# Chunked attention in a macaron block: probabilities laid by query block, whole-unit sums, two score units in a row, pool product in column halves

## The chip, the cores and the metric

The kernel runs as one program on all 8 cores of a Trainium2 chip. Each core works on 2,048 tokens of one of two sequences of 8,192, and on a halo of 512 tokens before them that it computes again; no core waits for another. The metric is the device time of the slowest core in microseconds (us).

## What is computed

One layer of a hybrid encoder block, D_MODEL 1024, with two feed-forward half steps around a mixer:

```
x = x + 0.5 * SwiGLU_1(RMSNorm(x))
h = RMSNorm(x);  u = h @ W_in          # pool channels (512) | q (512) | k (512) | v (512)
A = per-group trailing means (windows 2/4/8/16) - self, per-group 128x128 map (pool_w), per-channel scale
B = attention, 8 heads of 64, chunk of 64 queries over its own and the 8 previous chunks,
    scores * 64**-0.5 + clipped relative-position bias, softmax, @ v
merged = sigmoid(h W_g + b_g)[A] * (A @ W_bp) + sigmoid(h W_g + b_g)[B] * (B @ W_ba)
x = x + merged @ W_out
x = x + 0.5 * SwiGLU_2(RMSNorm(x));  out = RMSNorm(x)
```

A key block that lies before the start of the sequence counts for nothing in the softmax.

## The kernel before, in words

Activations are held transposed: channels on the 128 partitions, tokens along the free dimension, in 512-column halves `s` = 0, 1. A core does a halo tile H (512 tokens, only far enough to have keys, values and pool carry) and two tiles A and B of 1,024 tokens. Each tile goes through `ffn_up`, `ffn_down`, `w_in_phase`, `attention`, `gates_phase`, `w_out_phase`, `ffn_up`, `ffn_down`. Weights stream through a ring of five slots, loaded by POOL's queue and cast to bf16 on the way (`load_slot`). Every operation is recorded in program order by `Prog.op`, which also works out the waits: each engine then runs its own list strictly in the order in which it was recorded, and waits on semaphores for what its operation reads or overwrites. So the order in which the Python code calls things is the order on each engine.

**The attention stretch** (function `attention`, L906 on) is the place of the change. For each half `s` and each pair `p` of heads there are five units `u` (table `UNITS`), that is 40 units in a tile, taken in 8 rounds of five. A unit is 512 score columns for each of two heads `e`: one to two key blocks of 128 keys against 128 to 512 queries. Its steps:

- scores (`issue_S`, L927): for each head a matmul with 64 contraction rows, the two heads in the upper and lower half of the array's rows (form 64*128), into two of the PSUM banks 0 to 3 (`SB`, alternating by unit);
- the bias is added in place by DVE (L935) over 128 or 256 columns of each head;
- exp by ACT (L939), 1,024 columns, into one of four probability buffers (two in `Pt`, two in `ftmp`);
- for four of the five units DVE clears a 64x64 corner of each head (`issue_zero`, L947);
- products (`issue_PV`, L965): 64 output channels each for the two heads in the left and the right half of the array's columns (form 128*64). One matmul gives probabilities times values (bank 4), another gives the sums of the probabilities (bank 5), by 64 columns of ones that stand between the values of two heads in `Vt` (192 columns for a pair of heads). A key block of the halo has the flag of the halo (0 or 1) there instead of ones. After the fifth unit ACT takes Ln of the sums (L976) and Exp of its negative (L978), and one round later DVE multiplies (`divide`, L980).

In the gaps the same engine is given other work: the 16 products of the first gate (`gate` in `dense_chunks`, L878, in column halves 128*64), each cut in four chunks of four matmuls, `d(k)` issues `k` chunks. A gate accumulates in bank 6 or 7 (`DB`); its first chunk takes the bank by `nxt("dense", 2)`, which alternates; after its fourth chunk DVE copies the bank to SBUF (L884), and only then may the next user of that bank write. The eight products of the pool mixer (`pool_one`, `pool_w`, L400 form 128*128, with ACT's L849 behind) take a bank by the same alternation. `tick()` lets queued side work of DVE go.

`in_v` (L744 on) makes `Vt`: ACT copies the values (L747) and, before the change, ones or the flag (L750).

Of the kernel before, what the change touches and what calls it, by code (L numbers as in the profile page):

```python
# [26 lines left out]
VROW = 768  # L27
# [157 lines left out]
def build_nc():  # L185
# [12 lines left out]
    with es:  # L198
# [9 lines left out]
        Vt = sb("Vt", [128, KT_BLOCKS, VROW], BF16)  # L208
        biasT = sb("biasT", [128, 8, 256], F32)
# [18 lines left out]
        ones64 = cct[:, 384:448]  # L228
# [58 lines left out]
        B_cc = Buf("cc")  # L287
        B_g32 = Buf("g32")
# [446 lines left out]
        def in_v(mt, s, tb, sl):  # L735
            full = mt["full"]
            vs = (mt["blk0"] + s * 4 + tb) % KT_BLOCKS
            b = nxt("bank", NBANK)
            t0 = s * 512 + tb * 128
            mm_group(bank_ap(b),  # L740
                     [(hs[:, kc, t0:t0 + 128] if full else hh[:, kc, tb * 128:(tb + 1) * 128],
                       ring[:, sl, kc * 512:(kc + 1) * 512]) for kc in range(8)],
                     [(B_h[kc][s] if full else B_hh[kc]) for kc in range(8)] + [B_ring[sl]], b)
            vview = Vt[:, vs, :].rearrange("p (a c) -> p a c", c=192)  # L744
            vheads = Vt[:, vs, :].rearrange("p (a t d) -> p a t d", t=3, d=64)[:, :, 0:3:2, :]
            bview = bank_ap(b).rearrange("p (a e d) -> p a e d", a=4, e=2)
# [106 lines left out]
        UNITS = [([(-1, 0, 4)], (0, 128, 128), True),  # L853
# [51 lines left out]
        def attention(mt):  # L905
# [7 lines left out]
            def issue_S(i):  # L913
# [5 lines left out]
                def fn(t):  # L919
                    ins = None  # L920
                    pc = 0
                    for (dj, q0, nq) in segs:
                        col = ((base + dj) % KT_BLOCKS) * 128
# [5 lines left out]
                        pc += n  # L929
# [13 lines left out]
            def issue_zero(i):  # L943
                pi = state[i]
                if UNITS[units[i][2]][2]:
                    zap = P_aps[pi].rearrange("p (e t) -> p e t", e=2)[0:64, :, 448:512]
                    P.op("dve", lambda e: e.memset(zap, 0.0), writes=[B_P[pi]])  # L947

            def issue_PV(i):
# [4 lines left out]
                pap = P_aps[pi]  # L954

                def fn(t):
                    ins = None
                    pc = 0
                    for (dj, q0, nq) in segs:
                        vs = (base + dj) % KT_BLOCKS  # L960
                        n = nq * 128
                        for half in range(2):
                            for e in range(2):
                                l0 = p * 192 + (64 if half else 128 * e)
                                ins = t.matmul(ps[64 * e:64 * e + 64, (OB[half] * 512 + q0 * 128):(OB[half] * 512 + q0 * 128 + n)],  # L965
                                               Vt[:, vs, l0:l0 + 64], pap[:, e * 512 + pc:e * 512 + pc + n],
                                               start=(u == 0), stop=(u == 4), skip_group_check=True)
                        pc += n
                    return ins
                P.op("pe", fn, reads=[B_P[pi]] + [B_v[(base + dj) % KT_BLOCKS] for dj, _, _ in segs],  # L970
# [62 lines left out]
            issue_zero(n - 1)  # L1033
# [223 lines left out]
```

How the kernel before makes its waits and increments, by code:

```python
        def emit(engname, eng, tail=None):  # L1199
            for fn, waits, ev, is_dma in P.ops[engname]:
                for k, v in waits:
                    eng.wait_ge(sems[k], v)
                ins = fn(eng)
                ins.then_inc(sems[ev[0]], 16 if is_dma else 1)
            if tail is not None:
                tail(eng)
# [4 lines left out]
                def tail(e):  # L1211
                    for k in P.cnt:
                        if k.startswith("st"):
                            e.wait_ge(sems[k], P.cnt[k])
```

## Time and profile before

| what | value |
|---|---|
| median of 3 runs | 1517.97 us (1517.25 to 1522.94) |
| the profiled execution | 1512.99 us |
| its span on the slowest core (4) | 1511.4 us; other cores 1506.5 to 1511.1 |
| TensorE (PE) matmul busy | 1471.4 us, 97% |
| VectorE (DVE) busy | 540.9 us, 36% |
| ScalarE (ACT) busy | 462.7 us, 31% |
| chain that ended last | PE 91%, DMA 3%, DVE 3%, ACT 2% |

The busy time of PE comes from modelled ends of matmuls and includes pauses of a tenth of a microsecond; the starts of consecutive rows say more. A few matmul records are missing from a trace.

### The profile page before, as it was taken

What the parts mean: (1) busy time and instruction counts of PE and PEld (TensorE: products, weight loads), DVE (VectorE), ACT (ScalarE), POOL (GpSimd) and SP (SyncE); (2) the same over time, 40 slices, a digit from 0 to 9 for tenths busy, and PEclk for the clock granted to TensorE, in tenths of its full rate; (3) what the DMA queues carried; (4) which work ended last, traced back from release to release, by engine and by line L of the source; (5) the groups of instructions that cost most, each with busy time, mean ns of one, the idle gap of its engine ahead of it and who ended that gap; (6) DMA issues with size and microseconds to landing.
All of it is one profiled execution on the core that took longest, in us unless ns stands there. A gap on an engine that the chain in (4) does not pass through costs nothing.

```text
span 1511.4 us, 20500 instructions; the slowest of 8 cores (1506.5 to 1511.4 us)
## 1 busy us (share of the span) xinstructions
PE 1471.4 (97%) x7460; PEld 671.6 (44%) x7598; DVE 540.9 (36%) x872; ACT 462.7 (31%) x696; POOL 66.3 (4%) x129
## 2 busy tenths in 40 slices
PE   6999999999999999999999999999999999999997
PEld 2444444444444444444444444444444444444445
DVE  2323424222536554323245321223626555222124
ACT  3313112211358634213222311111357534111112
POOL 0000000000000000000000000000000000000000
PEclk9999999999999999999999999999999999999999
DMA  9853345998640454543264983344430643442323
GB/s 195 190 97 65 58 86 84 188 182 145 111 88 2 67 102 90 109 81 67 42 140 80 191 214 55 56 77 74 93 61 2 106 87 60 84 78 48 60 54 112
DMA packets 32482, 142.89 MB, mean 95 GB/s; under 512 B 2816, under 2 KB 5248, under 8 KB 21888
## 3 DMA queue, kind: packets, MB, share of 16 engines
q0 software_dynamic: 18000, 115.09, 43.3%
q1 hardware_dynamic: 14384, 26.48, 5.4%
q8 instruction: 63, 1.03, 0.3%
q14 instruction: 35, 0.29, 0.1%
HBM read 248.25 MB, written 8.39 MB: 170 GB/s over the span
## 4 chain that ended last, share of the span: by engine, by line
PE 91%; DMA 3%; DVE 3%; ACT 2%; issue 1%; another core or an unknown queue 0%; DVEq 0%; SPq 0%; ACTq 0%; POOLq 0%
PE ps L400 79%; PE ps L388 4%; PE ps L878 3%; DMA xs<-xT 2%; PE ps L965 2%; PE ps L927 1%; DMA ring<-wst 1%; DVE hs L505 1%; DVE ps L935 1%; ACT Pt L939 1%; PE ps L456 1%; ACT ftmp L939 0%; PE ps L433 0%; DVE ftmp L460 0%; DVE xs L662 0%
## 5 line engine op out<-in xcount | busy, mean ns | idle before, releaser
L400 PE MATMUL ps<-hs,ring 128*128 128x512 bf16 x3596 | 800.8, 380 | 6.1 <-DMA ring<-wst 2.2
L400 PEld LDWEIGHTS ps<-hs,ring 128*128 128x128 bf16 x3672 | 359.8, 98 | 437.6 <-issue 7.3
L400 PE MATMUL ps<-areg,ring 128*128 128x512 bf16 (+1 forms) x1953 | 426.4, 372 | 1.8
L585 DVE TENSOR_TENSOR areg<-ftmp,ps 128x512 bf16<-128x512 f32 x198 | 135.8, 687 | 524.3 <-PE ps L400 475.2
L400 PEld LDWEIGHTS ps<-areg,ring 128*128 128x128 bf16 x2004 | 195.7, 98 | 221.2 <-issue 1.0
L583 ACT ACTIVATE ftmp<-ps 128x512 f32<-128x512 f32 x198 | 118.2, 597 | 506.6 <-PE ps L400 475.1
L318 POOL DMA_DIRECT2D ring<-wst x125 | 66.1, 530 | 1386.5 <-PE ps L400 965.9
L599 DVE SCALAR_TENSOR_TENSOR xs<-ps,xs 128x512 f32<-128x512 f32 x69 | 47.6, 690 | 165.9 <-PE ps L400 134.1
L445 ACT ACTIVATE sqt<-xs 128x512 bf16<-128x512 f32 x56 | 35.2, 629 | 216.8 <-DVE xs L599 216.8
L935 DVE TENSOR_TENSOR ps<-ps,biasT 128x512 f32<-128x512 f32 (+1 forms) x80 | 46.9, 588 | 84.8 <-PE ps L927 84.8
L505 DVE SCALAR_TENSOR_TENSOR hs<-xs,cvt,rtmp 128x512 bf16<-128x512 f32 x80 | 54.6, 746 | 36.4 <-ACT rtmp L501 36.4
L878 PE MATMUL ps<-hs,ring 128*64 128x512 bf16 x512 | 67.5, 385 | 0.0
L422 ACT ACTIVATE sqt<-xs 128x512 bf16<-128x512 f32 x53 | 32.2, 626 | 73.7 <-DVE xs L1096 40.6
L939 ACT ACTIVATE Pt<-ps 128x1024 bf16<-128x1024 f32 x40 | 40.7, 1021 | 16.2 <-DVE ps L935 15.2
L388 PE MATMUL ps<-areg,ring 128*128 128x512 bf16 x202 | 45.2, 379 | 0.2
L939 ACT ACTIVATE ftmp<-ps 128x1024 bf16<-128x1024 f32 x40 | 40.8, 1020 | 14.3 <-DVE ps L935 13.6
L460 DVE TENSOR_TENSOR ftmp<-ftmp,sqt 128x512 f32<-128x512 f32 x45 | 31.0, 690 | 30.7 <-ACT sqt L445 30.5
L1071 ACT ACTIVATE ftmp<-ps,cvt 128x512 f32<-128x512 f32 x32 | 21.9, 685 | 58.9 <-PE ps L400 54.6
L388 PE MATMUL ps<-hs,ring 128*128 128x512 bf16 x132 | 33.9, 393 | 4.5 <-DMA ring<-wst 3.0
L927 PE MATMUL ps<-areg,Kt 64*128 64x384 bf16 (+3 forms) x256 | 31.1, 302 | 5.1 <-ACT Pt L939 2.6
L878 PEld LDWEIGHTS ps<-hs,ring 128*64 128x64 bf16 x512 | 23.5, 109 | 27.7 <-issue 14.6
L1076 DVE TENSOR_TENSOR areg<-ftmp,ps 128x512 f32<-128x512 f32 x32 | 22.0, 687 | 32.2 <-ACT ftmp L1071 28.2
(84 smaller groups left out, 617.5 us busy)
## 6 DMA issues: line engine op xcount, KB each, us to landing
ring<-wst POOLq DMA_DIRECT2D x81, 1024.0 KB, 8.6
ring<-wst POOLq DMA_DIRECT2D x40, 704.0 KB, 6.0
xs<-xT SPq DMA_DIRECT2D x3, 2048.0 KB, 23.0
outT<-xs SPq DMA_DIRECT2D x12, 512.0 KB, 22.5
areg<-xT SPq DMA_DIRECT2D x3, 1536.0 KB, 14.4
xs<-xT SPq DMA_DIRECT2D x8, 512.0 KB, 13.5
outT<-xs SPq DMA_DIRECT2D x8, 256.0 KB, 2.5
ring<-wst POOLq DMA_DIRECT2D x2, 512.0 KB, 9.3
```

What stands on the lines that cost most here:

```text
L318: return lambda e: e.dma_start(out=out, in_=in_)
L388: ins = t.matmul(out_ap, l, r, start=(i == 0), stop=(i == n - 1))
L400: ins = t.matmul(out_ap, l, r, start=(i == 0), stop=(i == n - 1))
L445: P.op("act", (lambda e: e.activation(out=sqt[:, qi, :], in_=src, func=AF.Square)), reads=[sbuf], writes=[B_sq[qi]])
L505: P.op("dve", (lambda e: e.scalar_tensor_tensor(out=dst, in0=src, scalar=cvt[:, gcol + kc:gcol + kc + 1], in1=rtmp[:, r * 512:(r + 1) * 51 ...
L583: P.op("act", (lambda e, bg=bg, ti=ti: e.activation(out=ftmp[:, ti, :], in_=bank_ap(bg), func=AF.Silu)), reads=[B_bank[bg]], writes=[B_tmp ...
L585: P.op("dve", (lambda e, bu=bu, ti=ti, j=j: e.tensor_tensor(out=a_ap(j, s), in0=ftmp[:, ti, :], in1=bank_ap(bu), op=ALU.mult)), reads=[B_t ...
L599: P.op("dve", (lambda e: e.scalar_tensor_tensor(out=xs[:, m, cols], in0=bank_ap(b), scalar=0.5, in1=xs[:, m, cols], op0=ALU.mult, op1=ALU. ...
L878: ins = t.matmul(ps[64 * e:64 * e + 64, b * 512:(b + 1) * 512], ring[:, sl[0], w0:w0 + 64], hs[:, kc, cols], start=(kc == 0), stop=(kc == 7))
L927: ins = t.matmul(bank_ap(b0 + e, n, pc), Kt[64 * e:64 * e + 64, p, col:col + 128], Q[64 * e:64 * e + 64, p, ql:ql + n], start=True, stop=True)
L935: P.op("dve", (lambda e: e.tensor_tensor(out=near, in0=near, in1=biasT[:, 2 * p:2 * p + 2, t0:t0 + nn], op=ALU.add)), reads=[B_bias], writ ...
L939: P.op("act", (lambda e: e.activation(out=P_aps[pi], in_=both, func=AF.Exp)), reads=[B_bank[b0], B_bank[b0 + 1]], writes=[B_P[pi]])
```

## The change

- `Vt` holds the values alone (128 columns for a pair of heads); `in_v` has one ACT copy instead of two. The sums use constants: `ones_bf`, or a new tile `hfl` with the halo's flag, filled once in tile H.
- `UNITS` is in another order (the unit of the block's own first keys comes last) and scores and probabilities lie at the column of their query block. The sums of a unit are then one matmul for each head over 512 columns, whatever its key blocks are; only where a halo block takes part (tile A, `s` = 0) they are split.
- The pool product is done in two column halves (128*64) instead of one 128*128 matmul.
- The loop over rounds issues in another order.

```diff
-            vview = Vt[:, vs, :].rearrange("p (a c) -> p a c", c=192)
...
-            P.op("act", (lambda e: e.activation(out=vheads, in_=bview, func=AF.Copy)),
+            P.op("act", (lambda e: e.activation(out=Vt[:, vs, :], in_=bank_ap(b), func=AF.Copy)),
                 reads=[B_bank[b]], writes=[B_v[vs]])
-            src = ones64 if full else hflagt
-            P.op("act", (lambda e: e.activation(
-                out=vview[:, :, 64:128], in_=src.unsqueeze(1).to_broadcast([128, 4, 64]), func=AF.Copy)),
-                reads=[B_cc], writes=[B_v[vs]])
...
+                P.op("act", lambda e: e.activation(out=hfl[:], in_=hflagt, func=AF.Copy), reads=[B_cc], writes=[B_hfl])
...
-            mm_group(bank_ap(b), [(ring[:, sl, g * 128:(g + 1) * 128], MX[:, g, cols])],
-                     [B_mx[g], B_ring[sl]], b)
+                for e in range(2):
+                    w0 = g * 128 + 64 * e
+                    ins = t.matmul(ps[64 * e:64 * e + 64, b * 512:(b + 1) * 512], ring[:, sl, w0:w0 + 64], MX[:, g, cols],
+                                   start=True, stop=True)
...
-        UNITS = [([(-1, 0, 4)], (0, 128, 128), True),
-                 ([(0, 0, 4)], (0, 256, 0), False),
-                 ([(1, 1, 3), (-4, 0, 1)], (0, 256, 0), True),
-                 ([(2, 2, 2), (-3, 0, 2)], (0, 256, 0), True),
-                 ([(3, 3, 1), (-2, 0, 3)], (0, 128, 0), True)]
+        UNITS = [([(-1, 0, 4)], (0, 128, 128), 448),
+                 ([(1, 1, 3), (-4, 0, 1)], (128, 256, 0), 64),
+                 ([(2, 2, 2), (-3, 0, 2)], (256, 256, 0), 192),
+                 ([(3, 3, 1), (-2, 0, 3)], (384, 128, 0), 320),
+                 ([(0, 0, 4)], (0, 256, 0), None)]
...
+                if any(flags):
+                    sums = [(q0 * 128, (q0 + nq) * 128, f) for (_, q0, nq), f in zip(segs, flags)]
+                else:
+                    sums = [(0, 512, False)]
...
             for i in range(0, n, 5):
-                if not i:
-                    d(1)
+                if i:
+                    issue_PV(i - 1)
                 else:
-                    pool_one()
+                    d(2)
                 issue_S(i)
+                issue_S(i + 1)
                 tick()
-                if i:
-                    issue_zero(i - 1)
-                    d(1)
-                    issue_PV(i - 2)
-                    issue_PV(i - 1)
-                issue_S(i + 1)
-                issue_zero(i)
-                tick()
-                d(2)
-                issue_S(i + 2)
                 if divide:
                     divide.pop(0)()
+                issue_zero(i)
+                d(4)
+                tick()
+                issue_S(i + 2)
+                issue_PV(i)
                 issue_zero(i + 1)
-                d(4)
-                issue_PV(i)
                 issue_S(i + 3)
+                issue_PV(i + 1)
                 issue_zero(i + 2)
                 tick()
                 d(1)
-                issue_PV(i + 1)
                 issue_S(i + 4)
+                issue_PV(i + 2)
                 issue_zero(i + 3)
-                issue_PV(i + 2)
                 tick()
-                if i == n - 5:
-                    pool_one()
+                d(3)
+                pool_one()
+                if i < n - 5:
+                    issue_PV(i + 3)
+                tick()
```

**Order on TensorE, before.** The middle of a round in tile A (L927 scores, L878 gate chunks, L965 products; `s_act` and `s_dve` are the engines waited for):

```order
L927 MATMUL ps<-areg,Kt 128x512 [waits s_act]
L927 MATMUL ps<-areg,Kt 128x512
L878 MATMUL ps<-hs,ring 64x512 x8
L927 MATMUL ps<-areg,Kt 128x384 [waits s_act]
L927 MATMUL ps<-areg,Kt 128x384
L927 MATMUL ps<-areg,Kt 128x128 x2
L878 MATMUL ps<-hs,ring 64x512 x16
L965 MATMUL ps<-Pt,Vt 64x512 [waits s_dve,s_act]
```

The four chunks in a row (x16) wait for nothing: the first ends one gate in one bank, the other three begin the next gate in the other bank.

**Order on TensorE, after.** The start of a round in tile A (L967 sums, L975 probabilities times values, L929 scores, L880 gate chunks):

```order
L967 MATMUL ps<-Pt,ones_bf 64x512 [waits s_act]
L967 MATMUL ps<-Pt,ones_bf 64x512
L975 MATMUL ps<-Pt,Vt 64x512 x2
L929 MATMUL ps<-areg,Kt 128x512 x2
L929 MATMUL ps<-areg,Kt 128x384 x2
L929 MATMUL ps<-areg,Kt 128x128 x2
L880 MATMUL ps<-hs,ring 64x512 x8
L880 MATMUL ps<-hs,ring 64x512 [waits s_dve]
L880 MATMUL ps<-hs,ring 64x512 x7
L929 MATMUL ps<-areg,Kt 128x256 [waits s_act]
```

The first product is the last unit of the round before. Two units of scores now stand together. The four chunks are now two that end a gate and two that begin the next, with a wait for DVE between them: since the pool product takes its bank between the begin of one gate and the next, both gates have the same bank.

**Order on DVE, after**, around the copy that this wait is for (L936 bias, L989 `divide`, L949 clearing, L886 copy of a gate), from the same round:

```order
L936 TENSOR_TENSOR ps<-ps,biasT 128x2x128 [waits s_pe]
L936 TENSOR_TENSOR ps<-ps,biasT 128x2x256 [waits s_pe]
L989 TENSOR_TENSOR areg<-ps,rtmp 128x512 [waits s_act]
L949 MEMSET ftmp 64x2x64 [waits s_act]
L886 COPY areg<-ps 128x512 [waits s_pe]
L936 TENSOR_TENSOR ps<-ps,biasT 128x2x256 [waits s_pe]
```

The copy stands behind the division of the pair before, which waits for ACT's Exp, and behind the clearing, which waits for exp of the round's first unit.

## Rows read from the trace of the kernel before

**Rows 1.** Windows, tile B's attention: length, busy by engine, PEclk, DMA share, GB/s.

```profile
1116.47:1184.18 67.71, 64.65 (x633) 28.48 (x640) 41.20 (x94) 51.65 (x63) 0.75 (x2) 1.00 0.09 17
```

**Rows 2.** Timeline, core 4, PE, one round: start, length, engine, line, operation.

```profile
460.43 0.39 PE L927 MATMUL ps<-areg,Kt 64*128 64x512 bf16 x2 [0.25 <-ACT Pt L939]
...
462.69 1.05 PE L878 MATMUL ps<-hs,ring 128*64 128x512 bf16 x8
463.67 0.39 PE L927 MATMUL ps<-areg,Kt 64*128 64x384 bf16 x4
463.99 1.92 PE L878 MATMUL ps<-hs,ring 128*64 128x512 bf16 x16
465.75 0.60 PE L965 MATMUL ps<-ftmp,Vt 128*64 128x512 bf16 x4
466.28 0.39 PE L927 MATMUL ps<-areg,Kt 64*128 64x256 bf16 x4
...
468.79 0.39 PE L927 MATMUL ps<-areg,Kt 64*128 64x512 bf16 x2 [0.25 <-ACT Pt L939]
```

**Rows 3.** Timeline, core 0, PE: the pool product between products and scores.

```profile
1139.94 0.63 PE L965 MATMUL ps<-Pt,Vt 128*64 128x384 bf16 x8
1140.50 0.39 PE L400 MATMUL ps<-areg,ring 128*128 128x512 bf16 x1
1140.82 0.39 PE L927 MATMUL ps<-areg,Kt 64*128 64x512 bf16 x2
```

**Rows 4.** Timeline, core 4, PE: two units of scores in a row, tile A's first round.

```profile
444.56 0.61 PE L927 MATMUL ps<-areg,Kt 64*128 64x512 bf16 x4 [0.29 <-ACT areg L726]
445.10 1.05 PE L878 MATMUL ps<-hs,ring 128*64 128x512 bf16 x8
```

**Rows 5.** Timeline, core 4, DVE, in the round of rows 2.

```profile
466.78 0.70 DVE L935 TENSOR_TENSOR ps<-ps,biasT 128x512 f32<-128x512 f32 x1 [0.72 <-PE ps L927]
467.49 0.17 DVE L947 MEMSET Pt<- 64x128 bf16 x1
467.58 0.62 DVE L884 COPY areg<-ps 128x512 f32<-128x512 f32 x1
```

**Rows 6.** Timeline, core 4, ACT, in the round of rows 2.

```profile
462.71 0.61 ACT L976 ACTIVATE rtmp<-ps 128x512 f32<-128x512 f32 x1
463.41 0.63 ACT L978 ACTIVATE rtmp<-rtmp 128x512 f32<-128x512 f32 x1
463.95 1.01 ACT L939 ACTIVATE ftmp<-ps 128x1024 bf16<-128x1024 f32 x1
```

**Rows 7.** Timeline, core 4, all engines, the end of tile A's attention.

```profile
509.39 2.13 ACT L939 ACTIVATE ftmp<-ps 128x1024 bf16<-128x1024 f32 x2 [1.58 <-DVE ps L935]
...
510.56 0.17 DVE L947 MEMSET ftmp<- 64x128 bf16 x1 [0.22 <-ACT ftmp L939]
...
510.88 0.63 PE L965 MATMUL ps<-ftmp,Vt 128*64 128x256 bf16 x8 [0.52 <-DVE ftmp L947]
...
513.27 0.63 PE L965 MATMUL ps<-ftmp,Vt 128*64 128x128 bf16 x8
...
514.00 0.60 ACT L976 ACTIVATE rtmp<-ps 128x512 f32<-128x512 f32 x1 [1.90 <-PE ps L965]
```

**Rows 8.** Groups of instructions: busy us, mean ns, idle before them.

```profile
L884 DVE COPY areg<-ps 128x512 f32<-128x512 f32 x32 | 20.8, 651 | 0.0
...
L750 ACT ACTIVATE Vt<-cct 128x256 bf16<-128x256 f32 x20 | 8.3, 417 | 1.8
```

**Rows 9.** Timeline, core 0, PE, near the start of the program.

```profile
47.04 3.52 PE L400 MATMUL ps<-hs,ring 128*128 128x512 bf16 x8 [2.34 <-DMA ring<-wst]
```

**Rows 10.** Core 0, windows, one microsecond of the same place (columns as rows 1).

```profile
48.00:49.00 1.00, 1.00 (x3) 0.30 (x2) 1.00 (x3) 0.00 (x0) 0.00 (x0) 0.50 1.09 180
```

**Rows 11.** Timeline, core 2, PE, at the same place.

```profile
47.13 3.18 PE L400 MATMUL ps<-hs,ring 128*128 128x512 bf16 x14 [1.95 <-DMA ring<-wst]
```

**Rows 12.** Core 2, windows, the same microsecond.

```profile
48.00:49.00 1.00, 1.00 (x6) 0.48 (x5) 0.93 (x2) 0.00 (x0) 0.00 (x0) 1.00 1.07 139
```

More of the change, by code:

```diff
@@ L26 @@
 KT_BLOCKS = 12
-VROW = 768
+VROW = 512
 SLOT_SIZES = {}
@@ L208, in build_nc @@
         Vt = sb("Vt", [128, KT_BLOCKS, VROW], BF16)
+        hfl = sb("hfl", [128, 64], BF16)
         biasT = sb("biasT", [128, 8, 256], F32)
@@ L227, in build_nc @@
         hflagt = cct[:, 320:384]
-        ones64 = cct[:, 384:448]
         ASUB = NJ * 512
@@ L287, in build_nc @@
         B_cc = Buf("cc")
+        B_hfl = Buf("hfl")
         B_g32 = Buf("g32")
@@ L743, in in_v @@
                      [(B_h[kc][s] if full else B_hh[kc]) for kc in range(8)] + [B_ring[sl]], b)
-            vview = Vt[:, vs, :].rearrange("p (a c) -> p a c", c=192)
-            vheads = Vt[:, vs, :].rearrange("p (a t d) -> p a t d", t=3, d=64)[:, :, 0:3:2, :]
-            bview = bank_ap(b).rearrange("p (a e d) -> p a e d", a=4, e=2)
-            P.op("act", (lambda e: e.activation(out=vheads, in_=bview, func=AF.Copy)),
+            P.op("act", (lambda e: e.activation(out=Vt[:, vs, :], in_=bank_ap(b), func=AF.Copy)),
                  reads=[B_bank[b]], writes=[B_v[vs]])
-            src = ones64 if full else hflagt
-            P.op("act", (lambda e: e.activation(
-                out=vview[:, :, 64:128], in_=src.unsqueeze(1).to_broadcast([128, 4, 64]), func=AF.Copy)),
-                reads=[B_cc], writes=[B_v[vs]])
             tick()
@@ L846, in pool_w, with fn @@
             cols = slice(s * 512, (s + 1) * 512)
-            mm_group(bank_ap(b), [(ring[:, sl, g * 128:(g + 1) * 128], MX[:, g, cols])],
-                     [B_mx[g], B_ring[sl]], b)
+            def fn(t):
+                ins = None
+                for e in range(2):
+                    w0 = g * 128 + 64 * e
+                    ins = t.matmul(ps[64 * e:64 * e + 64, b * 512:(b + 1) * 512], ring[:, sl, w0:w0 + 64], MX[:, g, cols],
+                                   start=True, stop=True)
+                return ins
+            P.op("pe", fn, reads=[B_mx[g], B_ring[sl]], writes=[B_bank[b]])
             P.op("act", (lambda e: e.activation(out=YP[:, g, cols], in_=bank_ap(b), func=AF.Identity,
@@ L920, in fn @@
                     ins = None
-                    pc = 0
                     for (dj, q0, nq) in segs:
+                        pc = q0 * 128
                         col = ((base + dj) % KT_BLOCKS) * 128
@@ L928, in fn @@
                                            Q[64 * e:64 * e + 64, p, ql:ql + n], start=True, stop=True)
-                        pc += n
                     return ins
@@ L944, in issue_zero @@
                 pi = state[i]
-                if UNITS[units[i][2]][2]:
-                    zap = P_aps[pi].rearrange("p (e t) -> p e t", e=2)[0:64, :, 448:512]
+                z = UNITS[units[i][2]][2]
+                if z is not None:
+                    zap = P_aps[pi].rearrange("p (e t) -> p e t", e=2)[0:64, :, z:z + 64]
                     P.op("dve", lambda e: e.memset(zap, 0.0), writes=[B_P[pi]])
@@ L954, in issue_PV @@
                 pap = P_aps[pi]
+                flags = [base + dj < 4 for dj, _, _ in segs]
+                if any(flags):
+                    sums = [(q0 * 128, (q0 + nq) * 128, f) for (_, q0, nq), f in zip(segs, flags)]
+                else:
+                    sums = [(0, 512, False)]
                 def fn(t):
                     ins = None
-                    pc = 0
+                    for c0, c1, flag in sums:
+                        for e in range(2):
+                            ins = t.matmul(ps[64 * e:64 * e + 64, OB[1] * 512 + c0:OB[1] * 512 + c1],
+                                           hfl[:] if flag else ones_bf[:, 0:64], pap[:, e * 512 + c0:e * 512 + c1],
+                                           start=(u == 0), stop=(u == 4), skip_group_check=True)
                     for (dj, q0, nq) in segs:
                         vs = (base + dj) % KT_BLOCKS
[L961 to L968, printed above, removed]
+                        c0, c1 = q0 * 128, (q0 + nq) * 128
+                        for e in range(2):
+                            l0 = p * 128 + 64 * e
+                            ins = t.matmul(ps[64 * e:64 * e + 64, OB[0] * 512 + c0:OB[0] * 512 + c1],
+                                           Vt[:, vs, l0:l0 + 64], pap[:, e * 512 + c0:e * 512 + c1],
+                                           start=(u == 0), stop=(u == 4), skip_group_check=True)
                     return ins
-                P.op("pe", fn, reads=[B_P[pi]] + [B_v[(base + dj) % KT_BLOCKS] for dj, _, _ in segs],
+                P.op("pe", fn, reads=[B_P[pi], B_ones, B_hfl] + [B_v[(base + dj) % KT_BLOCKS] for dj, _, _ in segs],
                      writes=[B_bank[b] for b in OB])
@@ L1024, in attention @@
                 d(1)
-                issue_PV(i + 1)
                 issue_S(i + 4)
+                issue_PV(i + 2)
                 issue_zero(i + 3)
-                issue_PV(i + 2)
                 tick()
-                if i == n - 5:
-                    pool_one()
+                d(3)
[3 more added lines that the diff above has]
+                tick()
             assert not dense and not pw
-            issue_zero(n - 1)
             rot["bank"] = 0
```

## The prediction

> **What bounds the kernel now.** Read the windows first. Over tile B's attention, 67.7 us long, TensorE's matmul rows are busy for 64.7 us, ACT for 51.7, DVE for 41.2, and the DMA share is 0.09 at a granted clock of 1.00 [rows 1]. So TensorE bounds this stretch, with ACT not far behind. Tile A's is alike; no other stretch gets other work on TensorE. Then read the timeline by starts, since lengths there hold a modelled tail. A round goes from one first score unit to the next, 460.43 to 468.79, 8.36 us [rows 2]. Sixteen matmuls of gate chunks take 1.76 us to the next start: 0.44 us a chunk, 0.22 us a pair of column halves. Eight take 0.98 us when scores follow, 0.10 over 0.88. A score unit takes 0.33 us to the next start, 0.22 of it columns [rows 2]. So each change between the forms 128\*64 and 64\*128 costs 0.10 us, ten times a round. A product over whole units takes 0.53 us with one such change, 0.43 without; a split one 0.56, so 0.46 without [rows 2, 3]. The sum for a round: 8 chunks 3.50, scores 5 x 0.22 = 1.10, products 2 x 0.43 + 3 x 0.46 = 2.24, pool product 0.32 with the change behind it [rows 3], changes 10 x 0.10 = 1.00, together 8.16; 0.2 us is left for waits. (The 0.25 us idle before a round's first scores on core 4 is no wait: core 0 has the pool product's record at that place, core 4 has lost it [rows 2, 3].)
>
> **What the change removes on TensorE.** Two score units in a row: one run of scores less, so two changes of form, 0.20 us a round. That such a pair works shows where one stands already: 0.54 us for both, 2 x 0.22 + 0.10 [rows 4]. The pool product in column halves goes at 0.22 where it took 0.32: 0.10 us. Whole-unit sums: three units lose a split of half their matmuls, 3 x 0.03 / 2, 0.04 us. TensorE's own work is then 3.50 + 1.10 + 2.20 + 0.22 + 8 x 0.10 = 7.82 us, 0.54 us less than a round has now. Were that all, 16 rounds would give 8.6 us.
>
> **What it adds.** The last order excerpts decide. Gates and the pool product share banks 6 and 7 by turns. Before, the pool product took its turn where no gate was open, and two gates that touch had different banks. Now it takes its turn inside an open gate, so the gate that begins in the middle of `d(4)` gets the bank of the gate that ended one instruction earlier. It must wait for DVE's copy of that bank, and the copy stands in DVE's queue behind the clearing of unit 0's corner, which waits for its exp, which stands in ACT's queue behind Ln and Exp of the pair before. I lay this out from the start of the pair's last product, t = 0:
>
> - product to Ln 0.73 [rows 7]; Ln to Exp 0.70; Exp to exp 0.54 [rows 6]: t = 1.97. The scores and bias of unit 0 are ready by then: change at 0.43, scores at 0.53, bias 0.50 later [rows 2, 5], 0.7 at most and 0.1 to ACT.
> - exp 1.02, to the clearing 0.15 (509.39 + 1.02 to 510.56) [rows 7]: t = 3.14.
> - clearing to copy 0.09 [rows 5]; copy 0.65 [rows 8]; DVE to TensorE 0.15 (510.56 + 0.17 to 510.88) [rows 7]: t = 4.03.
>
> TensorE gets there at 0.43 + 0.10 + 0.44 + 0.10 + 2 x 0.44 = 1.95. It waits 2.08 us, with all its later work of the round queued behind. Nothing covers that.
>
> Behind the wait the round goes on: two chunks, change, scores of unit 2 at 5.01; its bias runs 5.51 to 6.21, its clearing to 6.38, TensorE hears at 6.53 and would have come at 6.18 (scores, product, scores with their changes): 0.35 us more. Unit 4's scores wait for unit 2's exp, 6.31 to 7.33: no row prices ACT to TensorE alone, I bound it by 0 and by DVE's 0.15, and take 0.15: nothing to 0.05. The pool product waits for the copy of the gate that ends in `d(3)`: bias of unit 4 to 8.8, clearing, the gate's end at 8.8 plus 0.28 (0.50 of scores to bias less 0.22), copy to 9.73, heard at 9.88 where TensorE would be at 9.68: 0.2. So a round is 7.82 + 2.08 + 0.35 + 0.2 = 10.45 us, 2.1 us more than now. The exp of units 3 and 4 come in time for their products.
>
> Seven of the eight rounds of a tile have the long wait (in the first no pair is being finished and the first two gates have different banks): 7 x 2.1 = 14.7. The first round gains 0.5, and the wait of 0.52 us for a clearing at the end [rows 7] goes, since a chunk and the pool product now lie before that product. So +13.7 us a tile, +27.4 us for both. Tile A has split sums and leftover pool side work on DVE in its first round; from 0 to the length of one bias, 0.7 us [rows 5]; I take 0.3.
>
> **What costs nothing.** ACT's 20 copies of ones, 8.3 us [rows 8], fall in `in_v`, where TensorE has a bank rotation of five and waits for none of them; one small copy comes. The weight loads keep their order, and 0.09 of DMA share [rows 1] leaves room. Exp, bias and clearing keep count and size.
>
> **Sum.** Against the profiled execution: 1513.0 + 27.7 = 1540.7 us. That execution was 5.0 us under the median of the runs shown, 1518.0. The measured number will be such a median: 1518.0 + 27.7, about 1545 us. What a measurement of this kernel can tell from no change is some 0.5%, 7.6 us.
>
> **Bounds.** Unknown are the small hops and how far DVE and ACT overlap neighbours (the copy starts 0.08 us before the end of the clearing ahead of it [rows 5]). Low: 1.9 us for the long wait and 0.1 for the others, a round of 9.85, 1.5 more than now: 2 x (10.5 - 1) = +19, 1532 to 1537 by either base. High: 2.2 and 0.8, a round of 10.8: +33, 1551.
>
> **Rivals.**
>
> *The clock falls in the waits.* Near the start, core 0 stood 2.34 us and the clock fell to half, 0.50 [rows 9, 10]; core 2 stood 1.95 us at the same place and kept 1.00 [rows 11, 12]. The new waits, 2.1 us, lie between the two. Each fall would cost what core 0's did: eight matmuls in 3.5 us, 0.44 each instead of 0.22, 1.7 us. If half of the 14 waits bring one, +12 us: 1557; all, 1569. For: the size. Against: the work around each wait is dense, and the wait is on the near side of the middle. The Trainium skill (TensorE: Matmul & The Clock Gate, A second HAM failure mode: psum-queue depth-cycling) describes this very pattern, matmul groups that pause for PSUM banks in each iteration and a clock that goes to and fro; by it I would have the clock fall in many rounds. The trace of before has no such fall in attention, but no such wait either. Chance 0.24.
>
> *No measurable loss.* If the copy could go as soon as its gate has ended (0.28 + 0.65 + 0.15 = 1.08 us of wait), that is if unit 0's exp were over 0.9 us before that gate's end has reached DVE, a round would be 7.82 + 1.08 = 8.90, +0.54: 14 x 0.54 less 1.8 is +6, 1524 us, within the 7.6. The point is t = 2.0 for the clearing; the layout has 3.14, and even without Ln and Exp ahead the exp would end at 2.6. The Trainium skill (TensorE: Matmul & The Clock Gate, Architectural detail) calls the queues of ScalarE and VectorE strictly first in, first out; by that rule the copy can't overtake, and the order of starts in rows 5 and 6 agrees. Chance 0.05; a tenth of it, and hops much shorter still, would make it faster: 16 x -0.54 is -8.6, 1509, only if the bank cost nothing at all.
>
> *The change doesn't do what it says:* the column halves of the pool product, or sums with a constant, run one after the other instead of side by side. Then 0.22 us for each product pair, up to 16 x 6 x 0.22 = +21 us on top, 1566. Gate chunks and products run in pairs now, and their form is the same; chance 0.04.
>
> **How the numbers follow.** Forecast 0.67, clock 0.24, no loss 0.05, form 0.04. Predicted is the forecast's 1545. The range starts at the lower bound, 1535, and reaches to 1562, into the clock rival past its half: outside are the no-loss case, most falls of the clock, and the form: under 0.2. Slower by over 0.5%: 0.67 + 0.24 + 0.04, and nothing of the no-loss case: 0.95; within 0.5% 0.04; faster 0.01.
>
> **What would show it.** In the changed profile: the gate line (L880) with some 2 us idle before it 14 times, released by DVE's copy L886; rounds of 10.3 to 10.6 us; attention stretches of about 81.5 us at a clock of 1.00; scores twice a round in one run of 0.54 us; the pool product (L847) 0.22 us to the next start. A fall of the clock would stand as 0.5 in parts of the rounds. The forecast is wrong if the gate line waits under 1.5 us, or if rounds come out under 9.5 us.

## The result, and the profile after

The changed kernel takes 1550.38 us in the median of 4 runs (1548.81 to 1554.49), against 1519.40 us for the kernel before in runs beside it (1517.25 to 1522.94): a ratio of 1.0207, 95% interval 1.0193 to 1.0221, so +31.0 us. The profiled execution took 1549.45 us, its span is 1547.8 us on core 4, and the other cores have 1537.9 to 1547.8 us at mean clocks of 0.990 to 0.996 (0.997 to 0.999 before). In some executions the cores of one die run longer at a lower granted clock; the ratios leave these out, the kernel of experiment 5 is shown by its other execution, and one kernel of experiment 8 only by cores 4 to 7, which were spared.

First, the waits of TensorE on core 4: engine, line, what released it, then us in total, times, and the longest.

```profile
PE ps L880 <- DVE areg L886: 26.6, 14, 2.3
```

This group stood at 0.0 on the gate line before. Fourteen waits of 1.90 us in the mean, released by the copy L886, are the long wait of the prediction, in number and place. The group on the page has them as the idle time after the bar:

```profile
L880 PE MATMUL ps<-hs,ring 128*64 128x512 bf16 x512 | 68.8, 389 | 26.6 <-DVE areg L886 26.6
```

Then one round on TensorE (timeline, core 4: start, length, engine, line, operation), from first scores to first scores, as in [rows 2]:

```profile
1189.36 0.61 PE L929 MATMUL ps<-areg,Kt 64*128 64x512 bf16 x6
1189.90 1.05 PE L880 MATMUL ps<-hs,ring 128*64 128x512 bf16 x8
1192.80 1.05 PE L880 MATMUL ps<-hs,ring 128*64 128x512 bf16 x8 [1.84 <-DVE areg L886]
1193.78 0.39 PE L929 MATMUL ps<-areg,Kt 64*128 64x256 bf16 x4
...
1194.66 0.39 PE L929 MATMUL ps<-areg,Kt 64*128 64x128 bf16 x4
1195.31 0.41 PE L967 MATMUL ps<-ftmp,ones_bf 128*64 128x512 bf16 x2 [0.25 <-DVE ftmp L949]
...
1197.07 1.46 PE L880 MATMUL ps<-hs,ring 128*64 128x512 bf16 x12
1198.62 0.41 PE L847 MATMUL ps<-areg,ring 128*64 128x512 bf16 x2
1198.84 0.41 PE L967 MATMUL ps<-Pt,ones_bf 128*64 128x512 bf16 x2
...
1199.83 0.61 PE L929 MATMUL ps<-areg,Kt 64*128 64x512 bf16 x6
```

The round is 1199.83 - 1189.36 = 10.47 us, where 8.36 stood before. Two score units and the way to the gate take 0.54, the pool product 0.22. The chunks at 1189.90 would have ended 0.88 us later, at 1190.78; the next ones start at 1192.80. So TensorE stands 2.02 us; the profile says 1.84 since it lets a matmul end some 0.17 us later than the next could start.

DVE and ACT in the same round tell why (timeline, core 4). The last product of the pair before starts at 1188.80, which is t = 0:

```profile
1189.52 0.60 ACT L985 ACTIVATE rtmp<-ps 128x512 f32<-128x512 f32 x1 [0.18 <-PE ps L975]
1190.22 0.63 ACT L987 ACTIVATE rtmp<-rtmp 128x512 f32<-128x512 f32 x1
1190.75 1.01 ACT L940 ACTIVATE Pt<-ps 128x1024 bf16<-128x1024 f32 x1
1190.95 0.69 DVE L989 TENSOR_TENSOR areg<-ps,rtmp 128x512 bf16<-128x512 f32 x1
...
1191.91 0.17 DVE L949 MEMSET Pt<- 64x128 bf16 x1 [0.27 <-ACT Pt L940]
1192.00 0.65 DVE L886 COPY areg<-ps 128x512 f32<-128x512 f32 x1
```

DVE is idle before the clearing and waits for exp. The copy, whose gate has long ended, stands behind it; it ends at 1192.65 and TensorE starts 0.15 us later.

The stretch in windows, tile B on core 4 (columns as [rows 1]):

```profile
1136.05:1219.53 83.48, 67.22 (x606) 28.52 (x607) 43.18 (x95) 52.47 (x63) 0.70 (x2) 0.98 0.07 14
```

The length is 83.5 us instead of 67.7 (0.2 of it since this core has lost the record of the first matmul behind the stretch), ACT and DVE have the work they had, and the clock reads 0.98. It was below 1.00 in parts of a round, one microsecond each on core 4:

```profile
1160.00:1161.00 1.00, 1.00 (x12) 0.38 (x8) 0.00 (x0) 0.00 (x0) 0.00 (x0) 1.00 0.00 0
1161.00:1162.00 1.00, 1.00 (x8) 0.16 (x4) 0.72 (x2) 0.00 (x0) 0.00 (x0) 0.57 0.00 0
1162.00:1163.00 1.00, 1.00 (x8) 0.32 (x8) 0.36 (x2) 0.94 (x1) 0.00 (x0) 0.50 0.00 0
1163.00:1164.00 1.00, 1.00 (x10) 0.47 (x6) 0.38 (x2) 0.78 (x2) 0.00 (x0) 0.50 0.00 0
1164.00:1165.00 1.00, 1.00 (x8) 0.24 (x6) 0.01 (x1) 0.33 (x1) 0.00 (x0) 0.72 0.06 16
```

The wait before it is that of 1159.78 (`[2.14 <-DVE areg L886]`). The clock falls to the lower of the two levels (1.2 of 2.4 GHz) for some 3.4 us and then is full again. Over the eight cores there are 23 such falls behind 112 long waits, 2 to 4 on a core. The waits are not all alike: by the profile's idle time 80 of the 112 are 1.84 us long (5 falls), 16 in tile A 1.90 (8 falls), and 16 in tile B 2.13 and 2.26 (10 falls). A round with a fall is 1.16 to 1.22 us longer than the same round on a core without one, mostly 1.21. Core 7 has one fall in each tile, with stretches of 83.12 and 83.25 us; without it they would be 81.9 and 82.0.

### The profile page after: what moved, and what is told of

Same layout as the page of the kernel before. It is cut to its first block, busy times and chain, and to the rows that moved or that the text cites. A ratio compares the mean times of both kernels' runs of the same rounds, so it can differ in the third digit from the quotient of the medians.

```text
span 1547.8 us, 20305 instructions; the slowest of 8 cores (1537.9 to 1547.8 us)
## 1 busy us (share of the span) xinstructions
PE 1482.8 (96%) x7419; PEld 673.6 (44%) x7542; DVE 544.5 (35%) x872; ACT 456.5 (29%) x677; POOL 66.3 (4%) x129
## 4 chain that ended last, share of the span: by engine, by line
PE 90%; DMA 3%; issue 2%; DVE 2%; ACT 2%; DVEq 0%; SPq 0%; ACTq 0%; POOLq 0%
PE ps L401 78%; PE ps L389 4%; PE ps L880 3%; DMA xs<-xT 2%; PE ps L967 1%; DMA ring<-wst 1%; PE ps L975 1%; PE ps L929 1%; DVE hs L506 1%; DVE areg L886 1%; PE ps L457 1%; ACT Pt L940 1%; ACT ftmp L940 1%; ACT rtmp L985 1%; PE ps L434 0%
## 5 line engine op out<-in xcount | busy, mean ns | idle before, releaser
L880 PE MATMUL ps<-hs,ring 128*64 128x512 bf16 x512 | 68.8, 389 | 26.6 <-DVE areg L886 26.6
L936 DVE TENSOR_TENSOR ps<-ps,biasT 128x512 f32<-128x512 f32 (+1 forms) x80 | 45.8, 590 | 104.8 <-PE ps L929 104.7
L880 PEld LDWEIGHTS ps<-hs,ring 128*64 128x64 bf16 x512 | 27.2, 111 | 50.4 <-issue 37.6
L1101 DVE TENSOR_TENSOR xs<-ps,xs 128x512 f32<-128x512 f32 x32 | 22.1, 692 | 27.1 <-PE ps L401 24.6
```

The costliest lines, as they stand in the source:

```text
L880: ins = t.matmul(ps[64 * e:64 * e + 64, b * 512:(b + 1) * 512], ring[:, sl[0], w0:w0 + 64], hs[:, kc, cols], start=(kc == 0), stop=(kc == 7))
L936: P.op("dve", (lambda e: e.tensor_tensor(out=near, in0=near, in1=biasT[:, 2 * p:2 * p + 2, t0:t0 + nn], op=ALU.add)), reads=[B_bias], writ ...
```

## The experiments

Theory 1 is the prediction's: both gates have one bank, and its copy is late behind the clearing. The rivals are the other parts of the change (layout, sums, column halves, two score units) and the clock. Lengths of a stretch go from its first gate chunk to the first full matmul of the gates phase, 67.8 us in tile A and 67.7 in tile B before. The kernel before took 1513.29 us in the median beside experiments 1 to 3 and the first kernel of 8, 1514.76 beside 4 to 7, and 1514.32, in one execution, beside the other two of 8. The changed kernel did not run beside them, so it is compared with them by the ratios to the kernel before.

**1. The pool product takes no turn.** It uses the bank that the gate which just ended leaves.

```diff
-                    pool_w(slw, g, s, DB[nxt("dense", 2)])
+                    pool_w(slw, g, s, DB[rot["dense"]])
```

> The changed kernel, but the pool product uses the bank of the next gate without taking a turn in the alternation, so that the two gates that touch have different banks again. Theory 1 (the loss is the bank shared by two gates that touch): the gate line waits for DVE's copy no more, the rounds of 10.46 us come down by about 1.8 to 8.6-8.8 us, the attention stretches to 69-71 us, and no fall of the clock is left in them (granted clock of the cores 0.997 or more): 1521 to 1527 us, still some us slower than before (67.7 us a stretch), since exp of a round's first unit stands behind Ln and Exp. Theory 2 (the new order as such, with ACT's chain, makes the round long, and the wait would only move to another line): rounds stay above 10 us, another line waits 1.5 us or more, 1545 us or more.

1517.89 us, ratio 1.0046 (1.0014 to 1.0079). The stretches are 69.8 and 70.0 us. The round, on core 6's timeline of TensorE (the last row of a view can be cut short by its window, here and below):

```profile
1146.06 0.61 PE L929 MATMUL ps<-areg,Kt 64*128 64x512 bf16 x6
1146.60 1.92 PE L880 MATMUL ps<-hs,ring 128*64 128x512 bf16 x16
1148.71 0.40 PE L929 MATMUL ps<-areg,Kt 64*128 64x256 bf16 x4 [0.20 <-ACT ftmp L940]
...
1149.59 0.39 PE L929 MATMUL ps<-areg,Kt 64*128 64x128 bf16 x4
1150.27 0.41 PE L967 MATMUL ps<-Pt,ones_bf 128*64 128x512 bf16 x2 [0.29 <-DVE Pt L949]
...
1152.04 1.46 PE L880 MATMUL ps<-hs,ring 128*64 128x512 bf16 x12
1153.59 0.41 PE L847 MATMUL ps<-areg,ring 128*64 128x512 bf16 x2
...
1154.79 0.39 PE L929 MATMUL ps<-areg,Kt 64*128 64x512 bf16 x2
```

The four chunks are one run again (x16) and nothing stands between them. The round is 8.73 us; no wait of L880 is left, and no fall of the clock. By the two ratios, 1.0207 and 1.0046, some 24 of the 31 us hang on who has which bank. The round is still longer than 8.36, though TensorE has only 7.82 us of work in it. By the starts it stands 0.25 us before the scores of unit 2, for exp, 0.35 before the product of unit 1, for a clearing, and 0.24 before the pool product.

**2 and 3. The copy's place in DVE's queue.** In the first, the clearing goes behind the gate's chunks and their copy; in the second, the copy stands ahead of the division too.

```diff
                 if divide:
                     divide.pop(0)()
-                issue_zero(i)
                 d(4)
+                issue_zero(i)
```

```diff
                 tick()
+                d(4)
                 if divide:
                     divide.pop(0)()
                 issue_zero(i)
-                d(4)
```

> The changed kernel with the clearing of unit 0's corner issued behind the four chunks instead of ahead of them: the copy of the gate then stands on DVE behind the division alone. If the place in DVE's queue sets the length of the wait, the copy starts when the division has ended, about 0.45 us earlier: waits of 1.4 us instead of 1.84, rounds of 10.0 us, about 1543 us, and fewer falls of the clock. If the wait is for TensorE's own end of the gate or for something else, it stays at 1.84 us.

> The changed kernel with the four chunks issued ahead of both the division and the clearing: nothing stands before the copy on DVE but the two biases. If the place in the queue sets the wait, it falls to the gate's end plus 0.28, the copy 0.65 and 0.12 to TensorE: 1.05 to 1.1 us, rounds of 9.7 us, stretches of 76 to 77 us, and, if waits of 1.84 us were what made the clock fall, no fall in them: 1535 to 1539 us. If the bank rule were not the cause, no change.

One execution each: 1535.68 us with stretches of 79.0 and 78.7, and 1528.64 us with 75.7 and 75.1. In the first kernel the waits before the gate come to 20.3 us in 14, 1.45 each. They are put down to a clearing, as here on core 0, in the longest of them (the other 13 are 1.43 to 1.49):

```profile
1149.56 0.69 DVE L989 TENSOR_TENSOR areg<-ps,rtmp 128x512 bf16<-128x512 f32 x1 [0.35 <-ACT rtmp L987]
1150.17 0.68 DVE L886 COPY areg<-ps 128x512 f32<-128x512 f32 x1
1150.82 0.17 DVE L949 MEMSET ftmp<- 64x128 bf16 x1
...
1151.00 0.41 PE L880 MATMUL ps<-hs,ring 128*64 128x512 bf16 x2 [1.72 <-DVE ftmp L949]
```

The clearing touches nothing that the gate's matmul uses; the copy ends at 1150.85, 0.15 us before the start, as in the kernel after. What ended last on the engine named is not always what was waited for. In the second kernel (core 5) the copy starts as soon as its gate has ended:

```profile
1145.46 0.69 DVE L886 COPY areg<-ps 128x512 f32<-128x512 f32 x1 [0.17 <-PE ps L880]
...
1146.29 0.41 PE L880 MATMUL ps<-hs,ring 128*64 128x512 bf16 x2 [0.95 <-DVE areg L886]
```

What is left is the least that one bank for two gates costs, 0.96 us in the profile's terms. The two places in DVE's queue are thus worth about 0.45 and 0.49 us of the 1.90 in the profile's terms. Neither kernel has a fall of the clock in a long wait. All three kernels came in under the times expected, which reckoned from the 1519 us of the first comparison; against the kernel before beside them, these two are at +22.4 and +15.4 us.

**4. The parts without the order.** The layout, whole sums, order of units and pool halves of the change, with the order of the rounds before (the pool product ahead of the scores, where no gate is open).

> The changed kernel's probabilities by query block, whole-unit sums with constants, new unit order and pool product in column halves, but the round issued in the order of the kernel before. Theory 1 (the loss is all in the order of the round, through the shared bank and ACT's chain): no wait at the gate line, rounds of 8.2 to 8.4 us, stretches of 66.5 to 68 us, within 4 us of before. Rival (the new layout or the sums cost TensorE or DVE time of their own, e.g. by 64-column constants that are loaded anew for each unit): rounds of 8.6 us or more.

1514.44 us, ratio 0.9999 (0.9989 to 1.001); stretches 67.3 us, rounds 8.30 us. These parts cost nothing that can be measured, and what they bring, about 1 us in both tiles, can't be told from nothing in the time.

**5. The pool product in halves alone,** in the kernel before.

```diff
-            mm_group(bank_ap(b), [(ring[:, sl, g * 128:(g + 1) * 128], MX[:, g, cols])],
-                     [B_mx[g], B_ring[sl]], b)
+                for e in range(2):
+                    w0 = g * 128 + 64 * e
+                    ins = t.matmul(ps[64 * e:64 * e + 64, b * 512:(b + 1) * 512], ring[:, sl, w0:w0 + 64], MX[:, g, cols],
+                                   start=True, stop=True)
```

> The kernel before with the pool product in column halves alone. By the prediction's term it saves the 0.10 us that the change to the form 128*128 costs, once a round: the start of the pool product to the start of the scores 0.32 us as before, of which 0.10 is now the change to the scores, and 0.10 less from the product ahead to the pool product; rounds of 8.26 instead of 8.36 us, stretches of 66.9 instead of 67.7 us. If column halves of it ran one after the other: 0.12 us more a round.

A miss: 1515.21 us, and the stretches stay at 67.8 and 67.7 us. Timeline, core 6, TensorE and one row of ACT:

```profile
1142.20 1.02 ACT L946 ACTIVATE Pt<-ps 128x1024 bf16<-128x1024 f32 x1 [1.58 <-DVE ps L942]
1142.53 0.63 PE L972 MATMUL ps<-Pt,Vt 128*64 128x384 bf16 x8
1142.99 0.38 PE L852 MATMUL ps<-areg,ring 128*64 128x512 bf16 x2
1143.37 0.39 PE L934 MATMUL ps<-areg,Kt 64*128 64x512 bf16 x2
```

From the product to the pool product it is 0.46 us where it was 0.56 [rows 3], so the change of form is gone. But from there to the scores it is 0.38, where the halves and one change make 0.32 and the 128\*128 product also took 0.32 [rows 3]: the first scores of a round come when exp has freed their banks, not when TensorE is ready. The exp that reads these banks (of the unit two before) ends at 1143.22, 0.15 us before they start.

**6. No open gate at the pool product's turn.** The changed kernel without the two chunks at the start of the first round.

```diff
                 if i:
                     issue_PV(i - 1)
-                else:
-                    d(2)
```

> The changed kernel without the two gate chunks ahead of its first round (they come at the end of the last round instead). Every round then ends a gate just before the pool product, no gate is open when that takes its turn, and gates that touch have different banks, with the alternation as it is. Theory 1: the same as taking the turn away: no wait of over 1 us at the gate line, rounds of 8.6 to 8.8 us, stretches of 68.5 to 70.5 us, 3 to 6 us over before, clock 0.997 or more. If it is the order of the round and not the parity of the banks: as changed, 30 us over before.

1516.71 us, ratio 1.0015 (1.0005 to 1.0025); rounds 8.46 us, a little under what was expected, no wait of L880, no fall. The stretches are 67.0 and 67.4 us, but here the first scores lie ahead of the first chunk; from the scores on it is 67.5 and 68.6. With two chunks less in front, the gates begin and end at other places, the pool product takes its turn between two gates, and gates that touch have different banks. The two gates with the pool product between them share one, but they lie 1.7 us apart, long enough for the copy. A second, independent edit takes the cost away.

**7. A better order.** The changed parts with exp of the first unit ahead of Ln and Exp of the pair before, the gates' chunks in another cut and the pool product without a turn.

```diff
-                    pool_w(slw, g, s, DB[nxt("dense", 2)])
+                    pool_w(slw, g, s, DB[rot["dense"]])
             for i in range(0, n, 5):
+                d(1)
                 if i:
-                    issue_PV(i - 1)
-                else:
-                    d(2)
+                    pool_one()
                 issue_S(i)
-                issue_S(i + 1)
                 tick()
+                if i:
+                    issue_PV(i - 2)
+                d(1)
+                if i:
+                    issue_PV(i - 1)
+                d(1)
+                issue_S(i + 1)
+                issue_S(i + 2)
                 if divide:
                     divide.pop(0)()
                 issue_zero(i)
-                d(4)
                 tick()
-                issue_S(i + 2)
-                issue_PV(i)
+                d(5)
                 issue_zero(i + 1)
+                issue_PV(i)
                 issue_S(i + 3)
-                issue_PV(i + 1)
                 issue_zero(i + 2)
                 tick()
-                d(1)
                 issue_S(i + 4)
-                issue_PV(i + 2)
                 issue_zero(i + 3)
+                issue_PV(i + 1)
+                issue_PV(i + 2)
                 tick()
-                d(3)
-                pool_one()
-                if i < n - 5:
-                    issue_PV(i + 3)
-                tick()
+                if i == n - 5:
+                    pool_one()
```

> A new order of the round on the changed kernel's layout: pool product without a turn in the alternation; units 1 and 2, and units 3 and 4, with their scores in a row (three runs of scores a round instead of five or four); the pair's last two products early in the next round but behind unit 0's scores, so that unit 0's exp stands ahead of Ln and Exp on ACT; five gate chunks in a row behind the scores of units 1 and 2. If the changes of form and the ACT chain are what is left, TensorE's own work is 3.50 + 1.10 + 2.20 + 0.22 + 6 x 0.10 = 7.62 us and small waits some 0.3: rounds of 7.9 to 8.1 us, stretches of 64.5 to 66 us, 3 to 6 us less than before. If ACT or DVE queues bite elsewhere, rounds of 8.4 us or more and no gain.

1509.48 us, ratio 0.9967 (0.9954 to 0.998): faster than before by 5 us, and by the two ratios (1.0207 and 0.9967) some 36 us faster than the changed kernel. The order and the pool product's turn were changed together, so no part has a price of its own. Stretches are 65.1 and 65.3 us; the round goes from 1142.48 to 1150.44 on core 5, 7.96 us:

```profile
1142.48 2.35 PE L880 MATMUL ps<-hs,ring 128*64 128x512 bf16 x20
...
1150.44 0.84 PE L880 MATMUL ps<-hs,ring 128*64 128x512 bf16 x6
```

**8. How falls go with the length of the wait.** Three kernels make the copy later by repeating it, with the same result in the copy's target: every gate's copy twice; only that of the half `s` = 0, which is the late one, twice; a piece of 128 columns ahead of the latter. The second diff is against the first, the others against the changed kernel.

```diff
-                            P.op("dve", lambda e: e.tensor_copy(out=za_ap(m, s), in_=bank_ap(b)),
-                                 reads=[B_bank[b]], writes=[B_za[m][s]])
+                            for _ in range(2):
+                                P.op("dve", lambda e: e.tensor_copy(out=za_ap(m, s), in_=bank_ap(b)),
+                                     reads=[B_bank[b]], writes=[B_za[m][s]])
```

```diff
-                            for _ in range(2):
+                            for _ in range(2 - s):
```

```diff
+                            if s == 0:
+                                P.op("dve", lambda e: e.tensor_copy(out=za_ap(m, s)[:, 0:128], in_=bank_ap(b, 128)),
+                                     reads=[B_bank[b]], writes=[B_za[m][s]])
```

> The changed kernel with each gate's copy done twice (the same result). Theory 1: the long wait grows by one copy to 2.4-2.5 us, the pool product's wait by up to 0.57 us, so rounds of 11.5 us without falls of the clock, stretches of 89 us, 1565 us; if the length of a wait decides on the fall of the clock, falls come in most of the seven rounds instead of one or two, each 1.3 us: 1575 to 1585 us and a clock of 0.98. If falls came by chance and not by the length of the wait, one or two a stretch as now.

> The changed kernel with the copy done twice only for every second gate, the one that ends in front of the long wait (the same result). The long wait is then as in the run with all copies doubled, 2.5 to 2.7 us, but the pool product's wait stays at 0.1 to 0.2 us instead of 0.9. If the length of the one long wait decides on the clock, as many falls as there, 80 to 100 of 112 waits (8 cores, 14 each); if the sum of the pauses in a round decides, clearly fewer, 40 to 70. Rounds of 11.2 us without a fall; 1560 to 1570 us.

> The changed kernel with a copy of 128 columns ahead of the copy of every second gate (the same result): the long wait 2.05 to 2.2 us instead of 1.84. If the chance of a fall goes up with the length of the wait between 0 of 112 at 1.45 us, 23 at 1.84 and 91 at 2.69, some 35 to 60 falls; if it has a fixed threshold under 1.84 us with chance in it, 23 or so. Rounds of 10.7 us without a fall; 1545 to 1555 us.

One execution each: 1579.84 us with every copy doubled and 1554.76 us with the piece; of the second kernel only the spans of cores 4 to 7 count, 1557.3 to 1560.3 us. The waits of TensorE, in the order of the diffs (the second on core 4):

```profile
PE ps L880 <- DVE areg L887: 37.6, 14, 3.0
PE ps L847 <- DVE areg L887: 12.5, 14, 1.0
```

```profile
PE ps L880 <- DVE areg L887: 37.3, 14, 2.9
```

```profile
PE ps L880 <- DVE areg L889: 31.7, 14, 2.5
```

All kernels with a shared bank in one table, the falls counted in windows of one microsecond:

| kernel | mean long wait, us (profile's idle) | falls / long waits |
|---|---|---|
| copy ahead of the division | 0.96 | 0 / 112 |
| copy behind the division | 1.45 | 0 / 112 |
| the change | 1.90 | 23 / 112 |
| piece of 128 columns more | 2.26 | 44 / 112 |
| late copy doubled | 2.66 | 27 / 56 |
| every copy doubled | 2.69, and 0.89 before the pool product | 91 / 112 |

Falls become more frequent with the wait. The last two rows have nearly the same long wait and differ in the second one of each round, and the share goes from 48% to 81% (45 of 56 on the same four cores). So, by one execution of each, the other pauses count too. Nor are the falls independent: with the late copy doubled, only 2 of the 27 come in the round right behind another.

## Why the prediction was right, and where not

**Which engine bounds.** Right. What TensorE stands is not hidden: the stretches grew by what seven rounds grew by.

**The bank and the queue.** Right, and shown. Giving each gate its own bank, in two ways (experiments 1 and 6), removes the wait and 24 to 29 us. Moving the copy up in DVE's queue (experiments 2 and 3) removes half of it in two steps. The Trainium skill (TensorE: Matmul & The Clock Gate, Architectural detail) has the queues of ScalarE and VectorE strictly first in, first out; the copy at 1192.00 behind an idle DVE agrees.

**The layout of the long wait.** From t = 0: Ln at 0.72 (0.73 said), Exp 0.70 behind it (0.70), exp 0.53 (0.54), clearing at 3.11 (3.14), copy 0.09 later (0.09), TensorE at 4.00 (4.03), which was ready at 1.98 (1.95). So 2.02 us, where 2.08 was said.

**The small waits.** Product of unit 1: 0.65 us behind the scores instead of 0.33, so 0.32 (0.35 said). Pool product: the three chunks ahead of it (12 matmuls) take 1.55 to its start instead of 1.31, so 0.24 (0.2). Scores of unit 4: 0.02 (0 to 0.05). Together with the long wait the round is 10.47 (10.45).

**The savings of 0.54 us a round.** By the prediction's own rows TensorE's work falls from 8.16 to 7.82, so only 0.34 of them are work; the other 0.20 are the waits that a round had before, taken as gone without a reason. They don't go: with the shared bank undone a round is 8.73, not 7.82. For the forecast this did no harm, since it laid out the waits of the new round one by one. Experiment 7 shows that another order can have most of it: 7.96.

**The sum.** Without falls the stretches are 81.9 and 82.0 us (about 81.5 said): +14.1 in tile A, where 13.7 + 0.3 was summed, and +14.3 in tile B, where it was 13.7. Seven rounds give 7 x 2.11 = 14.8. In tile B two of them are 0.30 and 0.42 longer at full clock too, and the first round and the end give back 1.2 (1.0 said).

**The clock.** This is the term that was mis-sized: the forecast had no fall, the rival had half of 14 or all. 2 to 4 came on a core, 23 in 112 waits. And a fall costs 1.21 us, not 1.7. The round with a fall on core 4 shows where the rest is:

```profile
1162.06 0.61 PE L929 MATMUL ps<-areg,Kt 64*128 64x128 bf16 x4
1162.60 0.64 PE L967 MATMUL ps<-ftmp,ones_bf 128*64 128x512 bf16 x2
```

The product of unit 1 no longer waits for its clearing, which had cost 0.32 at the full clock: 1.7 - 0.32 = 1.38, most of the way.

On core 4, with three falls, that is 3 x 1.21 = 3.6 us of its +36.4 us of span. The Trainium skill (TensorE: Matmul & The Clock Gate, A second HAM failure mode: psum-queue depth-cycling) gives the pattern; here a fifth of the rounds follow it. The number on record, 1545, is 5.4 us under 1550.4: the kernel before read 1.4 us more in this comparison than in the runs shown, 0.7 was rounded away, and 3.3 are left. Falls of 2 to 4 x 1.21 = 2.4 to 4.8 us could cover them, and so could the dips to 0.81 below; those executions have no trace, so it isn't shown. Profile against profile the forecast is further off: 1513.0 + 27.7 = 1540.7, measured 1549.45. That the number on record is closer comes in part from its base, 5.0 us above the profiled execution.

**The other rivals.** No measurable loss: its point was a clearing by t = 2.0; it came at 3.11. The change not doing what it says: the halves of a sum or of the pool product run side by side, 0.22 us from 1198.62 to 1198.84.

**What stays open.** Core 4's +36.4 us of span are 28.4 in the two attention stretches without their falls, 3.6 for the falls, 0.8 before the stretches, 1.3 behind, and 2.2 between them, where the change does nothing. Cores 0 to 3 have 605.0 us between the stretches, as before; cores 4 and 5 have 2.2 us more, cores 6 and 7 3.9. Their clock reads under full at the same times, as in these windows of core 5 (20 us, and 1 us in it), where before it read 1.00:

```profile
540.00:560.00 20.00, 20.00 (x91) 8.86 (x89) 11.91 (x18) 6.98 (x11) 0.53 (x1) 0.96 0.60 102
540.00:541.00 1.00, 1.00 (x6) 0.41 (x4) 0.69 (x1) 0.49 (x1) 0.00 (x0) 0.81 0.97 156
```

These are not falls like those behind the waits. The clock reads 0.81, not 0.50, for 5 to 8 us at a time, and TensorE stands nowhere near: eight matmuls in a row take 2.10 us where they take 1.73 at full clock ten microseconds later (core 5):

```profile
538.81 2.27 PE L401 MATMUL ps<-areg,ring 128*128 128x512 bf16 x8
540.91 2.27 PE L401 MATMUL ps<-hs,ring 128*128 128x512 bf16 x8
```

Between the stretches, cores 4 and 5 have 2 such dips and cores 6 and 7 have 4. What the windows read under full adds up to 2.4 us on core 5 and 4.2 on core 6, about what is missing there. Four cores at one time speaks for something of the die; no run here tells what brings it.

Also open are the two longer rounds of tile B (one is 1178.47 to 1189.36, 10.89 us, on core 4), at the same places on all eight cores. In the other, Ln starts 0.30 us later behind the product than elsewhere, and in this one the clearing starts 0.36 us later:

```profile
1156.51 0.60 ACT L985 ACTIVATE rtmp<-ps 128x512 f32<-128x512 f32 x1 [0.47 <-PE ps L929]
1181.38 0.17 DVE L949 MEMSET Pt<- 64x128 bf16 x1 [0.62 <-ACT Pt L940]
```

The late Ln stands in the kernels of experiments 2 and 3 too; why both are late, the traces do not show.

## What to carry to other kernels

When users of different kinds take turns on shared PSUM banks, write down for every round who gets which bank: a product moved into an open gate changes no instruction of the gates and cost 24 to 29 us here. Where two users must share a bank, look what stands ahead of the evacuating copy in its engine's queue, and put the copy there first. Fewer matmul columns or changes of form pay only if the engine that frees the next bank (here ACT's exp) is early enough, so change the order of that engine together with them. That is what experiments 1, 5 and 7 speak for; none of them changed the order of exp alone.

## What the runs showed of the hardware

A wait of TensorE near 2 us, again and again in a round of 10.5 us, brings a fall of its clock only now and then: 23 times in 112 at 1.90 us in the mean, never in 112 at 1.45 (8 of these were 1.72), 44 times in 112 at 2.26, 27 times in 56 at 2.66. Within the 112 of the changed kernel it was 5 of 80 at 1.84 us, 8 of 16 at 1.90 and 10 of 16 over 2.1. The same was seen with single waits near the start before, 2.34 us with a fall and 1.95 without [rows 9, 11]. Which of the waits bring one differs from core to core, though the cores run the same rounds. A fall lasted some 3.4 us at half clock and cost the round 1.16 to 1.22 us.

Apart from that, the granted clock of four cores of one die dipped to 0.81 for 5 to 8 us at about the same time, with no pause of TensorE near.

A change between the two half forms costs TensorE 0.10 us, and so does one between a half form and 128\*128 (0.56 against 0.46 us behind the products). Two column halves of 512 columns each, one in each half of the array, take 0.22 us together.
